# Attention in two mixer stages: the two heads of a partition pair are worked together, their score products in the two row halves of the array and their value products in alternating column halves

## The reference, cut to what matters

```python
# latent tokens, both layers: a 2-D neighbourhood plus all context keys
s_loc = einsum('bjqhd,bijkhd->bhjqik', q_r, k_b) * scale + bias
s_ctx = einsum('bjqhd,bchd->bhjqc', q_r, k_ctx) * scale
p = softmax(concatenate([s_loc, s_ctx]))
o = p_loc @ v_b + p_ctx @ v_ctx
# context tokens, first layer only: plain attention over 256 context keys
s = einsum('bqhd,bkhd->bhqk', q, k) * 64 ** -0.5
o = softmax(s) @ v
```

## Time and profile before

| | us |
|---|---|
| median of 3 runs | 3140.7 (3140.38 to 3141.37) |
| the profiled execution's own time | 3140.06 |
| its span in the trace | 3138.3 |
| first `Mix`, first score product to the product with `pool_w` | 575.7 to 655.1 |
| second `Mix`, the same | 1579.8 to 1631.7 |

### The profile page before, as it was taken

How to read it: one execution, slowest core, us unless ns; L and a number is a source line. 1 busy time by engine, 2 the same in 40 slices (tenths; PEclk the granted TensorE clock), 3 DMA queues, 4 the chain that set the end, 5 groups by cost and what they waited for, 6 DMA issues and landing times. The chain is left out here.

```text
span 3138.3 us, 47109 instructions
## 1 busy us (share of the span) xinstructions
PE 2926.0 (93%) x16182; PEld 2491.5 (79%) x16182; DVE 2188.5 (70%) x4187; ACT 1230.2 (39%) x2276; POOL 368.8 (12%) x412
## 2 busy tenths in 40 slices
PE   7999999999999999999999997688379999999998
PEld 4888888568888888888859996568268999999997
DVE  2888894558888975657556664455998777777775
ACT  2322233443222332223455454154025454444454
POOL 0111115000111100100400000000375000000000
PEclk9999999999999999999999998689559999999999
DMA  5555442123544454534415556004002555555553
GB/s 230 175 174 192 171 146 94 41 101 132 190 175 169 148 200 148 174 132 159 130 36 170 185 173 229 1 27 149 1 0 73 186 186 186 186 187 186 187 187 120
DMA packets 107708, 450.01 MB, mean 143 GB/s; under 512 B 11953, under 2 KB 12593, under 8 KB 94257
## 3 DMA queue, kind: packets, MB, share of 16 engines
q1 hardware_dynamic: 93744, 347.46, 34.3%
q0 software_dynamic: 13824, 100.67, 8.5%
HBM read 447.04 MB, written 1.05 MB: 143 GB/s over the span
## 5 line engine op out<-in xcount | busy, mean ns | idle before, releaser
L177 DVE TENSOR_TENSOR weight_lo<-weight_ring,weight_hi 128x512 fp32r<-128x512 f32 x1272 | 942.0, 746 | 553.6 <-ACT weight_hi L170 539.1
L170 ACT ACTIVATE weight_hi<-weight_ring 128x512 fp32r<-128x512 f32 x1272 | 798.6, 631 | 1204.8 <-PE bank L256 1203.5
L254 PE MATMUL bank<-operand_hi,weight_hi 128*128 128x256 f32 (+1 forms) x3168 | 1042.7, 329 | 24.0 <-DVE operand_lo L591 12.9
L256 PE MATMUL bank<-operand_hi,weight_lo 128*128 128x256 f32 (+1 forms) x3168 | 1035.7, 327 | 0.0
L255 PE MATMUL bank<-operand_lo,weight_hi 128*128 128x256 f32 (+1 forms) x3168 | 1035.6, 327 | 0.0
L254 PEld LDWEIGHTS bank<-operand_hi,weight_hi 128*128 128x128 f32 x3168 | 604.0, 191 | 89.0 <-issue 21.4
L255 PEld LDWEIGHTS bank<-operand_lo,weight_hi 128*128 128x128 f32 x3168 | 604.2, 191 | 53.8
L256 PEld LDWEIGHTS bank<-operand_hi,weight_lo 128*128 128x128 f32 x3168 | 604.1, 191 | 51.2
L846 DVE SCALAR_TENSOR_TENSOR extension_ffn<-extension_ffn,silu_c 128x512 f32<-128x512 f32 x532 | 392.9, 788 | 1.7
L254 PE MATMUL bank<-hidden_hi_ffn,weight_hi 128*128 128x512 f32 (+1 forms) x704 | 258.5, 367 | 2.0 <-DVE arena L1071 1.9
L256 PE MATMUL bank<-hidden_hi_ffn,weight_lo 128*128 128x512 f32 (+1 forms) x704 | 255.7, 363 | 0.0
(11 more groups left out here) (253 smaller groups left out, 2934.3 us busy)
## 6 DMA issues: line engine op xcount, KB each, us to landing
weight_ring<-in_ffn SPq DMA_DIRECT2D x272, 512.0 KB, 3.6
weight_ring<-in_experts SPq DMA_DIRECT2D x256, 512.0 KB, 3.5
extension_ffn<-in_w_mods POOLq DMA_DIRECT2D x96, 1024.0 KB, 7.1
weight_ring<-in_w_mix SPq DMA_DIRECT2D x56, 512.0 KB, 3.6
weight_ring<-in_w_second SPq DMA_DIRECT2D x52, 512.0 KB, 3.9
extension_mixer<-in_rel_bias SPq DMA_DIRECT2D x2, 1536.0 KB, 6.7
arena<-in_x SPq DMA_DIRECT2D x1, 2048.0 KB, 9.2
arena<-in_cmp_k SPq DMA_DIRECT2D x1, 2048.0 KB, 11.6
```

Source lines behind the costliest of these rows:

```text
L170: nc.scalar.activation(self.hi[:, g % 2, h], self.ring[:, g % NS, h], ACT.Copy).then_inc(self.rounded, 1)
L177: self.nc.vector.tensor_tensor(self.lo[:, g % 2, h], self.ring[:, g % NS, h], self.hi[:, g % 2, h].bitcast(F32), ALU.subtract).then_inc(se ...
L254: nc.tensor.matmul(out, a_hi, b_hi, start=start and n == 0, stop=False)
L256: last = nc.tensor.matmul(out, a_lo, b_hi, start=False, stop=stop and n == len(pairs) - 1)
```

## The change

The items are put in another order: the two heads of a pair for one query tile stand next to each other, so that items 2n and 2n + 1 are the two heads, and four items (4n to 4n + 3) are a pair of heads with both query tiles. One `scores(n)` now issues the score products of both heads, one in each row half, into two of four banks (0, 1, 6, 7). One `values(n)` now issues the value products of both heads, key tile by key tile, alternating between the two column halves of one bank, so there are half as many of them, each with twice the instructions. `pt` grows for that, and `move` takes all 128 partitions at once, half as often. PE's order is new as well: `scores(0)` and `scores(1)`, and then for each w `transposes(w)`; after it, at odd w, `scores(w // 2 + 2)`, which are items w + 3 and w + 4; and at w = 5, 9, 13 and so on `values(w // 4 - 1)`. DVE's order, and ACT's except for `move`, stay.

```diff
-        self.items = [(g, h, qt) for g in range(ng) for h in range(NA_H) for qt in range(2)]
+        self.items = [(g, 2 * hp + j, qt) for g in range(ng) for hp in range(NA_H // 2) for qt in range(2) for j in range(2)]
...
+    def score_bank(self, w):
+        return (0, 1, 6, 7)[w % 4]
...
-        def scores(w):
...
-            if w >= 2:
-                pe.wait_ge(self.scores_read.sem, self.scores_read.at(w - 1))
...
+        def scores(n):
+            if n >= 2:
+                pe.wait_ge(self.scores_read.sem, self.scores_read.at(2 * n - 2))
+            for w in (2 * n, 2 * n + 1):
+                g, h, qt = items[w]
+                lo, hi = keys(g)
+                po, q0 = 64 * (h % 2), g * S + qt * P
+                nc.tensor.matmul(chip.bank[self.score_bank(w)][:, 0:hi - lo], u[po:po + 64, CH_Q + h // 2, q0:q0 + P],
+                                 u[po:po + 64, CH_K + h // 2, lo:hi], start=True, stop=True)\
+                    .then_inc(self.scored.sem, 1)
...
         def values(n):
...
-            pe.wait_ge(self.copied.sem, self.copied.at(2 * n + 2))
+            pe.wait_ge(self.copied.sem, self.copied.at(4 * n + 4))
...
             for kt in range(nkt):
+                for j in range(2):
+                    h = items[4 * n + j][1]
+                    mm = nc.tensor.matmul(chip.bank[4 + n % 2][64 * j:64 * j + 64, 0:S],
+                                          v[:, kt + 4 - nkt, h * DH:(h + 1) * DH], self.turned_probs(n, j, kt),
+                                          start=(kt == 0), stop=(kt == nkt - 1))
...
-        for w in range(3):
-            scores(w)
+        scores(0)
         pe.wait_ge(evicted.sem, evicted.at(20))
+        scores(1)
         for w in range(len(items)):
-            if w + 3 < len(items):
-                scores(w + 3)
             transposes(w)
-            if w >= 2 and w % 2 == 0:
-                values(w // 2 - 1)
-        values(len(items) // 2 - 1)
+            if w % 2 and w // 2 + 2 < len(items) // 2:
+                scores(w // 2 + 2)
+            if w >= 5 and w % 4 == 1:
+                values(w // 4 - 1)
+        values(len(items) // 4 - 1)
```

More of the change, by code:

```diff
@@ L388 @@
 A_PT = A_SC + 2048
-A_POOL = A_PT + 2048
+A_POOL = A_PT + 4096
 A_MIXER = A_POOL + 2048 - A_WORDS
@@ L1170, in __init__ @@
         self.bias = chip.part(A_BIAS, NA_H, BIAS_ROWS * GRID)
-        self.sc, self.pt = chip.part(A_SC, 4, 512), chip.part(A_PT, 2, 4, S)
+        self.sc, self.pt = chip.part(A_SC, 4, 512), chip.part(A_PT, 8, 4 * P)
         self.ng = ng = 1 if last else 2
@@ L1182, in __init__ @@
             s.take(n) for s in (chip.scored, chip.scores_read, chip.maxed, chip.exped, chip.probs, chip.turned, chip.copied))
-        self.product, self.moved, self.mixed = chip.product.take(n // 2 + 1), chip.moved.take(n // 2), chip.mixed.take(1)
+        self.product, self.moved, self.mixed = chip.product.take(n // 4 + 1), chip.moved.take(n // 4), chip.mixed.take(1)
         self.y_there = chip.y_there.take(2)
@@ L1187, in keys, with turned_probs @@
         return (0, T2) if g == 0 else (S, T2)
+    def score_bank(self, w):
+        return (0, 1, 6, 7)[w % 4]
+    def turned_probs(self, n, j, kt):
+        return self.pt[:, 4 * (n % 2) + kt, :].rearrange("p (j q) -> p j q", j=2)[:, j, :]
     def sync(self, sp):
@@ L1232, in tensor @@
         evicted = self.mix_in.evicted
-        def scores(w):
-            g, h, qt = items[w]
-            lo, hi = keys(g)
-            po, q0 = 64 * (h % 2), g * S + qt * P
-            if w >= 2:
-                pe.wait_ge(self.scores_read.sem, self.scores_read.at(w - 1))
-            nc.tensor.matmul(chip.bank[w % 2][:, 0:hi - lo], u[po:po + 64, CH_Q + h // 2, q0:q0 + P],
-                             u[po:po + 64, CH_K + h // 2, lo:hi], start=True, stop=True)\
-                .then_inc(self.scored.sem, 1)
+        def scores(n):
[8 more added lines that the diff above has]
+                    .then_inc(self.scored.sem, 1)
         def transposes(w):
@@ L1254, in values @@
         def values(n):
-            g, h, _ = items[2 * n]
-            po = 64 * (h % 2)
-            pe.wait_ge(self.copied.sem, self.copied.at(2 * n + 2))
+            pe.wait_ge(self.copied.sem, self.copied.at(4 * n + 4))
             if n >= 2:
                 pe.wait_ge(self.moved.sem, self.moved.at(n - 1))
+            g, _, _ = items[4 * n]
             nkt = (keys(g)[1] - keys(g)[0]) // P
             for kt in range(nkt):
-                mm = nc.tensor.matmul(chip.bank[4 + n % 2][po:po + 64, 0:S],
-                                      v[:, kt + 4 - nkt, h * DH:(h + 1) * DH], pt[:, n % 2, kt, :],
-                                      start=(kt == 0), stop=(kt == nkt - 1))
+                for j in range(2):
[3 more added lines that the diff above has]
+                                          start=(kt == 0), stop=(kt == nkt - 1))
             mm.then_inc(self.product.sem, 1)
         pe.wait_ge(evicted.sem, evicted.at(16))
-        for w in range(3):
-            scores(w)
+        scores(0)
         pe.wait_ge(evicted.sem, evicted.at(20))
+        scores(1)
         for w in range(len(items)):
-            if w + 3 < len(items):
-                scores(w + 3)
             transposes(w)
-            if w >= 2 and w % 2 == 0:
-                values(w // 2 - 1)
-        values(len(items) // 2 - 1)
+            if w % 2 and w // 2 + 2 < len(items) // 2:
[3 more added lines that the diff above has]
+        values(len(items) // 4 - 1)
         pe.wait_ge(self.mixed.sem, self.mixed.at(1))
@@ L1297, in copies @@
             nkt = (keys(g)[1] - keys(g)[0]) // P
-            n = w // 2
+            n = w // 4
             act.wait_ge(self.turned.sem, self.turned.at(w + 1))
@@ L1301, in copies @@
                 act.wait_ge(self.product.sem, self.product.at(n - 1))
[L1302 removed]
+            at = S * (w % 2) + P * qt
+            nc.scalar.activation(pt[:, 4 * (n % 2):4 * (n % 2) + nkt, at:at + P],
                                  chip.bank[2 + w % 2][:, 0:nkt * P].rearrange("p (k q) -> p k q", q=P), ACT.Copy)\
@@ L1306, in move @@
         def move(n):
-            g, h, _ = items[2 * n]
-            po = 64 * (h % 2)
+            g, h, _ = items[4 * n]
             act.wait_ge(self.product.sem, self.product.at(n + 1))
-            nc.scalar.activation(y[po:po + 64, 4 + h // 2, g * S:(g + 1) * S], chip.bank[4 + n % 2][po:po + 64, 0:S],
+            nc.scalar.activation(y[:, 4 + h // 2, g * S:(g + 1) * S], chip.bank[4 + n % 2][:, 0:S],
                                  ACT.Copy).then_inc(self.moved.sem, 1)
@@ L1318, in scalar @@
             copies(w)
[L1319 to L1322, removed]
+            if w >= 6 and w % 4 == 2:
+                move(w // 4 - 1)
+        move(len(items) // 4 - 1)
+        act.wait_ge(self.product.sem, self.product.at(len(items) // 4 + 1))
         for b in range(2):
@@ L1333, in scale @@
             n = keys(g)[1] - keys(g)[0]
-            s, bank = sc[:, w % 4, :], chip.bank[w % 2]
+            s, bank = sc[:, w % 4, :], chip.bank[self.score_bank(w)]
             dve.wait_ge(self.scored.sem, self.scored.at(w + 1))
```

## The result

The changed kernel took 3163.0 us (median of 4, 3160.98 to 3163.23) against 3141.0 of the kernel before beside it: 22 us slower, ratio 1.0068, 95% interval 1.005 to 1.0085. Run a second time, beside the kernel before again, it took 3160.2 against 3139.6, ratio 1.0065 (1.0049 to 1.008). The forecast was 3156 with a range of 3143 to 3177.

What follows compares the result with a forecast made beforehand. The prediction took a loop between PE and DVE as the bound, not PE's busy share. Stage starts, 512-key loops, 256-key loops and the end summed to +15.1 us on 3140.06, giving 3156, range 3143 to 3177.

Steps and rivals of the forecast that it cites:

- Halves overlap: Score and value products: two halves run at once; a score pair takes 1.05 us, two heads' value products 1.88.
- The loop: Two items through PE and DVE: 5.84 us against 5.74 with 512 keys (7.23 at 1.2 GHz), 3.74 against 3.50 with 256.
- The start: Start of each mixer stage: transposes and scores come first at the low clock, so item 8 is 2.2 us late.
- Four loops from item 8, half at each clock: 512-key loops left in each layer, half at 2.4 GHz (+0.1) and half at 1.2 GHz (+1.5): +3.2 us per layer.
- 256 keys: Eight more loops in layer 0, half at +0.24 and half at +0.9 us: +4.6 us.
- The ends: Stage ends, one product of two heads instead of two of one: −0.3 us in layer 0, 0 in layer 1.
- the steady clock: Rival: the clock behaves as before, one 10 us fall at each stage start; +3.8 us, 3144; chance 0.16.
- Column halves that do not overlap: Rival: value products of two heads take 3.76 us, 7.2 at 1.2 GHz; 20 us more, 3176; chance 0.17.
- The rival on the other side: Rival: scores are there when DVE wants them, loops 4.03 and 2.58 us; 31 us less, 3110; chance 0.04.

Runs made afterwards that it cites:

- scores early: Changed kernel with the score pair issued at even w ahead of transposes(w) instead of at odd w behind it; 3118.5 us, ratio 0.993.
- filled: Changed kernel with useless products added on PE in the periods without value products; 3144.8 us, ratio 1.0011.
- values serial: Changed kernel with the two heads' value products one after the other instead of alternating; 3163.6 us, ratio 1.0068.
- early, spread, serial: Changed kernel with score pair ahead of transposes, value products cut in two by key tiles, heads one after the other in each part; 3111.8 us, ratio 0.9902.
- early and serial: Changed kernel with the score pair ahead of the transposes and the two heads' value products one after the other; 3128.8 us, ratio 0.9964.

## Why the prediction was right

The direction and the cause were right, and the size came near, in part because errors cancelled. Step by step:

- *Halves overlap*: 1.13 and 1.08 us as above. Score pair 1.05 to the next instruction, as costed. Right, also for the columns, where there was no row: 16 alternating instructions take 1.95 us at 2.4 GHz, 1.88 to the next. One of the two reasons for it was weak, since the projection's products are one instruction each and the fp32 products here two, so that their rates need not be alike.
- *The loop*: 5.84 forecast and measured at 2.4 GHz, 7.23 and 7.26 at 1.2 GHz, 3.74 and 3.74 with 256 keys. DVE's waits 1.80 and 3.21 for "1.8 and 3". Shown as the cause by "scores early", in which no wait for a score product is left.
- *The start*: item 8 was to be 2.2 us late. Counted from the first score product it begins at 25.9 us instead of 23.7 in both layers: +2.2 twice.
- *Four loops from item 8, half at each clock*: 3.2 forecast, 2.8 in layer 0 (25.3 for 22.5 us). In layer 1 three loops cost 1.4 and the end 1.7, together 3.1 against 3.2 and nothing for the end.
- *256 keys*: 4.6 forecast for eight loops, 2.0 measured for seven. The clock stayed at 2.4 GHz there for 17 us; half at each clock was too pessimistic, by about 2.
- *The ends*: −0.3 forecast for layer 0, +2.2 measured, and 1.7 more behind the stage. I had priced the lower clock at +2 and taken the other. Too optimistic, by 4.

The stages sum to 16.3 against 15.1, the 256-key loops and the ends being wrong in opposite ways: that these two come so close is luck. The larger miss is of a term that the sum did not have: in the profiled executions 6.6 of the 22.9 us lie outside the mixer stages, in code that nothing touched, 4.0 of them in the later attention. That most of the price is the clock is shown by "filled", where 16.3 became 3.0. The rivals: the steady clock (3144) did not come, but "filled" brought the mean clock of before back and measured 3144.8. Column halves that do not overlap were priced at 20 us. No run made such a kernel: "values serial" cost 4.3 in the stages, but its products still overlap in part, and the mean clock was no higher there (0.74 and 0.72 against 0.73 and 0.73). The rival on the other side (DVE the bound, 3110) came when the scores were issued early and the value products spread: 3107.9.

## What to carry to other kernels

When an engine's order is written by hand, follow each instruction that another engine waits for back to what stands ahead of it in its own queue: one call on the wrong side of a wait was worth 37 us in two stages here, and faster products on that engine saved nothing while it stood there. An experiment that is to take an overlap away has to be checked for whether it did: look up the duration of the products in it before its time is read as the price of the overlap. Work that is taken off PE also takes away what kept its clock up, so look at what PE does in the emptiest part of a period and spread the work before counting a saving; spreading alone gave nothing here as long as DVE waited for its scores. And compare stages, not totals alone: a stage that nobody touched can be off by several us and hide, or fake, a result of that size.

## What the runs showed of the hardware that was not expected

- Two row halves and two column halves both overlap for fp32 products: four score instructions take 1.13 us where two took 1.12, and eight value instructions for two heads take 1.08 where one head's eight took 1.94.
- Column halves overlap in part even when the written order does not alternate. With all of one head's instructions ahead of the other's, eight take 1.09 us ("early, spread, serial", at 597.10, where the first two start 0.01 us apart), and 16 take 2.86 ("early and serial", at 603.29) against 1.95 alternating (changed kernel, at 636.23). The rows do not say which instruction is whose. But one head's four take 1.08 by themselves, so eight in 1.09 can only be two heads' at once, and the second head's first instruction, the fifth in the written order, must have started beside the first one.
- Filler on PE made a kernel 17 to 18 us faster, 13.3 of them in the stages that were filled.
- The later attention stage took either 44.4 to 44.6 us or 50.0 to 50.1 in eleven profiles, never anything between (1.5 of the difference came back in the stage behind it), by where one fall of the clock lay. Its mean clock was 0.89 in the kernel before, 0.88 in "values serial" and 0.76 in the changed kernel.
